# An early weight stream capped at three units, with the input ahead of the bias rows

## The reference

```python
mod_l = (silu(c) @ w_mod + b_mod)            # six vectors of 1024: shift, scale, gate, ...
hl = rms_norm(x, norm1_g) * (1 + s1) + sh1   # 256 x 1024
u = hl @ w_pw1 + b_pw1                       # 1024 -> 2048
u = a * sigmoid(gate)                        # the two halves of u
# depthwise convolution of width 31, layer norm, silu, second product, MLP, second block
```

## Time and profile before

| | us |
|---|---|
| median of three runs | 1150.33 |
| lowest and highest | 1148.41, 1158.25 |
| the profiled execution | 1155.95 |
| its span, first to last instruction | 1153.8 |
| first matmul of TensorE | 17.56 |
| first product of pw1(0, 0) | 31.66 |
| first product of pw1(1, 0) | 77.51 |

### The profile page before, as it was taken

One profiled execution on the slowest core, in us unless ns is written; L12 is line 12 of the kernel. 1 busy time (PEld: TensorE's weight loads), 2 busy tenths in 40 slices (PEclk: granted clock), 3 DMA queues, 4 the chain that ended last, 5 costly groups with the idle time before them and its releaser, 6 DMA issues.

```text
span 1153.8 us, 14321 instructions
## 1 busy us (share of the span) xinstructions
PE 1065.4 (92%) x6112; PEld 904.0 (78%) x6112; DVE 589.8 (51%) x626; ACT 511.4 (44%) x609; POOL 26.2 (2%) x54
## 2 busy tenths in 40 slices
PE   3789999999996999898999999989998899999996
PEld 2555669998975998786888887779987778888875
DVE  2344345445436448646455555544575555545464
ACT  2243456444443445624444444543464454444442
POOL 1000000000002000000000000010000000000000
PEclk9899999999997999979999999989997999999998
DMA  8767596654441434034555556325230545555530
GB/s 339 255 224 272 187 412 234 207 204 163 159 158 53 163 119 147 1 115 168 187 187 189 199 186 211 135 86 173 102 110 0 210 146 183 183 184 194 187 111 36
DMA packets 30731, 195.52 MB, mean 169 GB/s; under 512 B 3552, under 2 KB 5638, under 8 KB 10698
## 3 DMA queue, kind: packets, MB, share of 16 engines
q1 hardware_dynamic: 30668, 194.61, 47.1%
HBM read 193.54 MB, written 2.04 MB: 170 GB/s over the span
## 4 chain that ended last, share of the span: by engine, by line
PE 83%; DVE 8%; ACT 4%; issue 3%; DMA 1%; POOL 0%; SPq 0%; POOLq 0%; ACTq 0%; DVEq 0%
PE ps L1344 56%; PE ps L1660 8%; PE ps L1696 2%; PE ps L1726 2%; PE ps L1396 2%; ACT hi L529 1%; PE ps L1811 1%; DMA raw<-stream 1%; DVE lo L903 1%; DVE scratch L1148 1%; PE ps L1870 1%; PE ps L1944 1%; PE ps L1377 1%; DVE xl L922 1%; PE ps L1732 1%
## 5 line engine op out<-in xcount | busy, mean ns | idle before, releaser
L903 DVE TENSOR_TENSOR lo<-raw,hi 128x2048 fp32r<-128x2048 f32 (+4 forms) x142 | 316.5, 2231 | 299.5 <-ACT hi L529 299.4
L529 ACT ACTIVATE hi<-raw 128x2048 fp32r<-128x2048 f32 (+4 forms) x142 | 264.2, 1864 | 183.4 <-PE ps L1344 163.2
L1344 PE MATMUL ps<-hi,xh 128*128 128x512 f32 (+3 forms) x672 | 261.9, 390 | 15.4 <-DVE xl L922 6.0
L1344 PE MATMUL ps<-hi,xl 128*128 128x512 f32 (+3 forms) x672 | 257.6, 383 | 0.0
L1344 PE MATMUL ps<-lo,xh 128*128 128x512 f32 (+3 forms) x672 | 257.4, 383 | 0.0
L1344 PEld LDWEIGHTS ps<-hi,xh 128*128 128x128 f32 x672 | 129.4, 193 | 48.5 <-issue 14.4
L1344 PEld LDWEIGHTS ps<-lo,xh 128*128 128x128 f32 x672 | 129.2, 192 | 23.7
L1344 PEld LDWEIGHTS ps<-hi,xl 128*128 128x128 f32 x672 | 129.5, 193 | 21.3
L1344 PE MATMUL ps<-hi,gh 128*128 128x512 f32 (+2 forms) x360 | 138.7, 385 | 4.3 <-DVE gl L1308 2.2
L1344 PE MATMUL ps<-hi,gl 128*128 128x512 f32 (+2 forms) x360 | 137.8, 383 | 0.0
L1344 PE MATMUL ps<-lo,gh 128*128 128x512 f32 (+2 forms) x360 | 137.6, 382 | 0.0
(11 more groups left out here) (265 smaller groups left out, 1275.9 us busy)
## 6 DMA issues: line engine op xcount, KB each, us to landing
raw<-stream SPq DMA_DIRECT2D x134, 1024.0 KB, 4.9
scratch<-stream SPq DMA_DIRECT2D x22, 1024.0 KB, 6.5
raw<-stream SPq DMA_DIRECT2D x8, 896.0 KB, 4.6
raw<-stream SPq DMA_DIRECT2D x4, 1008.0 KB, 4.8
raw<-stream SPq DMA_DIRECT2D x4, 876.0 KB, 5.1
raw<-stream SPq DMA_DIRECT2D x2, 864.0 KB, 4.7
raw<-stream SPq DMA_DIRECT2D x2, 768.0 KB, 4.3
raw<-stream SPq DMA_DIRECT2D x2, 672.0 KB, 5.4
```

The source lines that it names most:

```text
L529: nc.scalar.activation(hi[:, u["s"] % SPLIT_SLOTS, 0:n], raw_of(u, n), ACT.Copy).then_inc(S["hi_done"], 1)
L903: nc.vector.tensor_tensor(lo[:, slot, 0:n], raw_of(u, n), hi[:, slot, 0:n].bitcast(F32), ALU.subtract).then_inc(S["lo_done"], 1)
L1344: ins = nc.tensor.matmul(out, l, r, start=start and i == 0, stop=stop and i == 2, skip_group_check=skip)
```

## The change

SP issues x and ident directly behind the vectors, then unit 0; it waits until x has landed, and only then issues row_stack and units 1 and 2. From unit 3 up to the attention layers, each unit's issue also waits until the unit three places before it has landed. In the stream pw1(0, i) stands between mod(0, i) and mod(1, i). ScalarE and VectorE split pw1(0, i) before the columns of the same group. ScalarE makes xh directly from xnT, with scale and shift as its operands and one instruction per 128 columns; VectorE's xf stays for xl. TensorE does the second quarter of the next group after six products instead of twelve and its column sums after twelve instead of eighteen.

```diff
--- before.py
+++ after.py
@@ -53,6 +53,7 @@
 SLOT = 2048
 RAW_SLOTS = 4
 EARLY_SLOTS = 6
+IN_FLIGHT = 3
 SPLIT_SLOTS = 3
 LOOKAHEAD = SPLIT_SLOTS - 1
 NEG = -1.0e30
@@ -99,8 +100,8 @@
 
     for i in range(GROUPS):
         mod(0, i)
+        pw1(0, i)
         mod(1, i)
-        pw1(0, i)
     for i in range(3):
         pw1(1, i)
     mod(2, 0)
@@ -428,6 +429,10 @@
         def _(sp):
             def weights(units):
                 for u in units:
+                    if IN_FLIGHT <= u["index"] < units_of(("mla", 0))[0]["index"]:
+
+                        ahead = UNITS[u["index"] - IN_FLIGHT]
+                        sp.wait_ge(landed[ahead["slot"]], ahead["landed"])
                     old = u["before"]
                     if old:
                         if old["split"]:
@@ -456,12 +461,14 @@
                 row(lora_gain[:], f"lora{layer}", "in_lora")
 
             sp.dma_start(vec, vectors).then_inc(S["in_vec"], 16)
-            sp.dma_start(rows_raw, rows["stack"]).then_inc(S["in_rows"], 16)
-            sp.dma_start(ident, consts[:, C_ID:C_ID + P]).then_inc(S["in_ident"], 16)
             for b in range(NB):
                 sp.dma_start(h[:, b, :], x[b * P:(b + 1) * P, :]).then_inc(S[f"in_x{b}"], 16)
-            weights(UNITS[0:2])
-            weights(UNITS[2:3])
+            sp.dma_start(ident, consts[:, C_ID:C_ID + P]).then_inc(S["in_ident"], 16)
+            weights(UNITS[0:1])
+
+            sp.wait_ge(S["in_x1"], 16)
+            sp.dma_start(rows_raw, rows["stack"]).then_inc(S["in_rows"], 16)
+            weights(UNITS[1:3])
             weights(UNITS[3:7])
             sp.dma_start(rb, rel).then_inc(S["in_rel"], 16)
             sp.dma_start(hot, consts[0:BUCKETS + 1, C_HOT:C_HOT + HOT]).then_inc(S["in_rel"], 16)
@@ -575,8 +582,10 @@
 
             def group_high(i):
 
-                act.wait_ge(S["xf_done"], GROUP_KT * (i + 1))
-                nc.scalar.activation(xh[:, GROUP_KT * i:GROUP_KT * (i + 1), :], xf, ACT.Copy).then_inc(S["xg_hi"], 1)
+                act.wait_ge(S["cols_done"], 2 * (i + 1))
+                for k in range(GROUP_KT * i, GROUP_KT * (i + 1)):
+                    nc.scalar.activation(xh[:, k, :], xnT[:, k, :], ACT.Identity, scale=in_scale[:, k:k + 1],
+                                         bias=in_shift[:, k:k + 1]).then_inc(S["xg_hi"], 1)
 
             def gates(c):
                 for b in range(NB):
@@ -592,19 +601,20 @@
                 act.wait_ge(S["xnT_ps"], b + 1)
                 nc.scalar.activation(xnT[:, :, b * P:(b + 1) * P], ps[:, 2 * b:2 * b + 2, :].rearrange("p a (k m) -> p (a k) m", k=4),
                                      ACT.Copy).then_inc(S["xnT_ready"], 1)
+            feed(units_of(("pw1", 0))[0], 0)
             quarter_copy(1)
             group_high(0)
-            feed(units_of(("pw1", 0))[0], 0)
             for i in range(1, GROUPS):
                 quarter_copy(2 * i)
+                feed(units_of(("pw1", 0))[i], 0)
+                quarter_copy(2 * i + 1)
                 if i == 2:
                     act.wait_ge(S["rel_ps"], 1)
                     nc.scalar.activation(rel_row, ps[0:HD, 7, 0:HOT], ACT.Copy).then_inc(S["toep_done"], 1)
                 if i == 3:
                     wave_copy(0)
-                quarter_copy(2 * i + 1)
-                feed(units_of(("pw1", 0))[i], 0)
                 group_high(i)
+            feed(units_of(("pw1", 1))[0], 0)
             wave_copy(1)
             feed(units_of(("pw1", 1))[1], 0)
 
@@ -965,18 +975,16 @@
                 if i == 0:
                     dve.wait_ge(S["csb_done"], 2)
                     dve.wait_ge(S["xnT_ready"], NB)
+                feed(units_of(("pw1", 0))[i], 0)
                 columns(i)
                 dve.wait_ge(S["cols_done"], 2 * (i + 1))
                 for k in range(GROUP_KT):
                     kk = ks.start + k
                     nc.vector.tensor_scalar(xf[:, k, :], xnT[:, kk, :], in_scale[:, kk:kk + 1], in_shift[:, kk:kk + 1],
                                             ALU.mult, ALU.add).then_inc(S["xf_done"], 1)
-                if i:
-                    feed(units_of(("pw1", 0))[i], 0)
                 dve.wait_ge(S["xf_done"], GROUP_KT * (i + 1))
-                dve.wait_ge(S["xg_hi"], i + 1)
+                dve.wait_ge(S["xg_hi"], GROUP_KT * (i + 1))
                 nc.vector.tensor_tensor(xl[:, ks, :], xf, xh[:, ks, :].bitcast(F32), ALU.subtract).then_inc(S["xg_lo"], 1)
-                feed(units_of(("pw1", 0))[i], 0)
 
             for i in range(GROUPS):
                 group_input(i)
@@ -1502,7 +1510,13 @@
 
                     pe.wait_ge(S["quarter_sb"], 2 * i + 1)
                     quarters(2 * i + 2)
-                pw1_part(0, i, 0, (0, 1))
+                pw1_part(0, i, 0, (0,))
+                if i < GROUPS - 1:
+                    pe.wait_ge(S["quarter_sb"], 2 * i + 2)
+                    quarters(2 * i + 3)
+                pw1_part(0, i, 0, (1,))
+                if i < GROUPS - 1:
+                    column_sums(i + 1)
                 if i == 1:
                     pe.wait_ge(S["in_rel"], 32)
                     nc.tensor.matmul(ps[0:HD, 7, 0:HOT], rb, hot, start=True, stop=True).then_inc(S["rel_ps"], 1)
@@ -1514,13 +1528,7 @@
                 if i == 3:
                     pe.wait_ge(S["wave_done"], 1)
                     waves(1)
-                if i < GROUPS - 1:
-                    pe.wait_ge(S["quarter_sb"], 2 * i + 2)
-                    quarters(2 * i + 3)
-                pw1_part(0, i, 1, (0,))
-                if i < GROUPS - 1:
-                    column_sums(i + 1)
-                used(pw1_part(0, i, 1, (1,)), None)
+                used(pw1_part(0, i, 1, (0, 1)), None)
 
             pe.wait_ge(S["quarter_sb"], 8)
             pe.wait_ge(S["cols_done"], 2 * GROUPS)
```

## The result

The changed kernel takes **1144.23 us** (median of 9 runs, 1141.34 to 1151.54), the kernel before 1152.91 (9 runs); the ratio is 0.9934, 95% interval 0.9905 to 0.9962. By the ratio that is 7.6 us faster, within 1%, and by its interval 4.4 to 11.0 us; the two medians are 8.7 us apart. The forecast was 5 us and 1145.5.

A forecast was written before the change was run, and what follows sets the result against it. TensorE, busy 92%, bounds the kernel; at pw1(1, 0) first product +1.7, gaps -1.6, -1.6, -2.6, unit 8 +1.2, clock -1.6, lo -0.75 make -5.3, taken as -5 from 1150.33: 1145.5 us, range 1138 to 1153.

The forecast's parts named there:

- Input first is worth nothing by itself: Opening loads: x lands near 6.3 (14.9 before), TensorE's first quarter runs at 9 (17.56 before); alone worth nothing.
- The stack lands at 18.1: Row stack's DMA behind x: lands at 18.1, bounds 15 and 19.2; DVE waits for it before making xs.
- The gaps go: TensorE's idle before groups 1, 2 and 3 for xl (1.62, 1.62, 2.62 us) vanishes, with 2 us of cover.
- Unit 8 becomes the bound: Quarter 5 in group 1: TensorE reaches it at 46.1 and waits 1.2 us for unit 8, landing at 47.3.
- Where the slow engine now bites: Units behind the row stack on one DMA engine: 2.52 us each, taps 8.3, unit 7 at 44.8, unit 8 at 47.3.
- Its low clock: TensorE's group 3: the low clock that followed its gap goes, -1.6 us (4.58 - 3.00).
- The cap at nothing: SP's unit issues: at most three outstanding costs nothing, covered by 5 us of queued work.
- The sign of one sixteenth before 18: Opening DMA: a share of one sixteenth before 18 would show the forecast right.
- Rival A: Row stack's DMA: packets at 0.16, stack lands at 15; -8 us, so 1142; chance 0.17.
- B: Row stack is no plug, ident's small packets were slow; stack lands at 9.6, -15 us, so 1135; chance 0.07.
- C: Gaps go but TensorE stays at 1.2 GHz longer or in another low stretch; -0.6 us, 1150; chance 0.19.
- D: Slow DMA engine becomes the bound ahead of unit 8; at 0.37 per packet +2 us, 1152; chance 0.10.

The follow-up runs named there:

- e5: The kernel before with only SyncE's new order (x and ident first, wait for x, row stack, cap of three); ratio 1.0051.
- e7: The changed kernel with the one-operation form undone, xh again one copy of xf; ratio 0.9950 to the kernel before.
- e11: The changed kernel with TensorE's old order inside a group; ratio 0.9948 to the kernel before.
- e6: The changed kernel with VectorE making xs ahead of the bias rows, not waiting for the row stack; ratio 0.9975 to the kernel before.
- e8: The changed kernel with taps padded by one zero row, 31 to 32 rows; ratio 0.9913 to the kernel before.
- e1: The changed kernel without the cap on outstanding units, wait for x kept; ratio 0.9964 to the kernel before.
- e3: The changed kernel's engines and stream order with SyncE's old order, no wait for x, no cap; ratio 1.0008 to the kernel before.
- after_again: The changed kernel run once more, unchanged (the repeat); ratio 0.9971 to the kernel before.
- e10: The changed kernel with row stack of 48 rows, taps of 32 and xs ahead of the bias rows, both waits kept; ratio 0.9873 to the kernel before.

## Why the prediction was right

- *Input first is worth nothing by itself.* Shown, and worse than nothing (e5, with wait and cap: +3.2 us).
- *The stack lands at 18.1.* It was 17.0, in the repeat 17.5. First product forecast +1.7, measured +1.2. That it came so near is partly luck: the stack was 1.1 us early, but the column sums and the bias opening, which ran for the most part ahead of the low stretch before, now ran in it (1.86 us for 1.05, 2.07 for 1.52), a price of 1.4 us that I had left out.
- *The gaps go.* All three, and the 0.75 for lo. I gave ScalarE's new form 0.76; it takes 1.09, the upper bound, and nothing shows, as said. That its neighbour, the earlier split, did the work follows from e7 and e11, which each take one of the other parts out; the split itself was not undone alone.
- *Unit 8 becomes the bound.* Forecast a wait of 1.2 us, measured 1.41. e6 and e8 show from both sides that it is the bound. The size of the wait is luck: unit 8 landed 2.1 us earlier than forecast, and TensorE stood ready for it 2.2 us earlier (43.9 and not 46.1), 0.5 from the first product and 1.7 because group 0 took 8.3 us and not 10.0.
- *The term that was mis-sized* is in "Where the slow engine now bites": unit 8 at 47.3, landed 45.16. I put 0.27 us on most packets. In the changed kernel the 2 to 8 KB packets between 8.4 and 10.7 number 14 (27 less 13), 0.16 each, and between 11.5 and 15.8 they number 16 (33 less 17), 0.27 each; the last three lie between 15.85 and 16.35, 0.17 each. The view of its DMA for the first stretch:

```profile
DMA packets 127, 0.88 MB, mean 381 GB/s; under 512 B 13, under 2 KB 13, under 8 KB 27
```

and for the second:

```profile
DMA packets 222, 1.61 MB, mean 375 GB/s; under 512 B 17, under 2 KB 17, under 8 KB 33
```

  All 37 therefore took about 8 us and not 9.1; the 31 of taps were shorter too (unit 7 landed 10.8 us after unit 6, I had 11.6). These two make 1.9 of the 2.1 us by which the gain at pw1(1, 0) was 7.4 instead of 5.3: from unit 8's landing to pw1(1, 0) it was 25.0 us, about as in the forecast.
- *Its low clock.* Group 3 ran at full clock, as forecast, and group 0 recovered sooner (34.0 instead of 36.4), 1.7 us that the sum had at nothing ("group 0 as before 10.0 us"). All but 0.3 of it went into the wait: without it TensorE would have reached quarter 5 at 45.6, just behind unit 8.
- *The cap at nothing.* Nothing contradicts it: e1 shows no gain or loss outside the scatter. TensorE does lose 0.5 us to a DMA in a later stage, through ScalarE's wait at 141, which was one of the signs of being wrong; but two kernels without the cap lose 1.4 and 1.6 us at the same unit, and e6 with it none.
- *The sign of one sixteenth before 18* did not come as written: from 17.2 to 19.0 the DMA share is 0.12, two sixteenths.

Rival A (packets at 0.16) was half right; B, C and D did not come, though C's low stretches decide by how much one profiled run differs from another: its sentence that no run here shows this no longer holds, since the changed kernel has a low stretch at 151 in one profile and none in the other.

## To carry to other kernels

Look at the outermost size of every early DMA: one of 37 or 31 rows went through a single DMA engine and held up everything queued behind it, whichever place it had, and padding it to a multiple of 16 was worth more (5.55 us) than reordering SyncE's queue (a loss of 3.2) or the engines' programs and the stream (4.6), though less than the two together (7.36, in the repeat 6.46). When a landing comes far later than its bytes explain, look for a stretch whose DMA share is one sixteenth. And when a head start is gained on one engine, look at who waits next in program order, and at what later transfer will set the pace anyway; only a run that moves one and not the other tells. A wait that comes and goes between two kernels is no proof that their difference made it: look for the same wait in every other trace first.

## What the runs showed of the hardware

- The packets of a one-engine transfer came at 0.16 us between 8.4 and 10.7, at 0.27 between 11.5 and 15.8 and at 0.17 after that, with about the same traffic in all in the first two stretches (381 and 375 GB/s). So the load that I took as the cause is not it, as far as the GB/s tell; what is stays open.
- Long waits of TensorE for a unit went with the low clock during or right after them (5.5 us in e3, low from 44.0; 3.9 us in e6, low from 46.0), waits of 1.41 to 1.64 before quarter 5 or group 1 with none. But the wait's length alone does not settle it: around 150 a wait of 1.4 us was followed by 6.8 us of low clock in e3 and after_again, and one of 1.5 us in e10 by none.
- One program showed a low stretch of 6.8 us at 151 in one profiled execution and not in another. It cost 2.9 us, some 40% of what this change gave, and no edit made it.
- A unit of 1 MB, issued 8.7 us after unit 30 in every kernel, took 5.1 to 7.0 us to land, and 5.8 and 6.8 in two executions of one program. TensorE lost nothing to it at 5.1 and about 1.5 us at 6.8 to 7.0.
